# Attention probabilities of a hybrid trunk layer normalised by a scaled copy on ScalarE in place of VectorE's product

## The reference, cut to what matters

```python
s_lat = jnp.einsum('bcqhd,bckhd->bchqk', qb, k_blk) + bias      # 256 latent keys of the block
s_lat = jnp.where(mask, s_lat, NEG_INF)
s_ctx = jnp.einsum('bcqhd,bphd->bchqp', qb, k_ctx)              # 128 context keys
p = jax.nn.softmax(jnp.concatenate([s_lat, s_ctx], axis=-1), axis=-1)
o = einsum(p[..., :n_keys], v_blk) + einsum(p[..., n_keys:], v_ctx)
```

## Time and profile before

| what | value |
|---|---|
| median of 3 runs | 1238.8 us (1236.86 to 1239.94) |
| the profiled execution, its own time | 1235.06 us |
| its span, first to last instruction | 1233.2 us |
| busy over the span: PE, DVE, ACT, POOL | 91%, 73%, 55%, 21% |
| mean granted TensorE clock | 0.955 of 2.4 GHz |
| PtHi L1040 / PtLo L1437 / products L1448 | 80 each, mean 446 / 498 / 749 ns |

### The profile page before, as it was taken

The page is one execution under the profiler, slowest core; times in us unless marked ns, Lnnn a source line. Parts: engine busy times, 40 slices in busy tenths (PEclk is TensorE's granted clock), DMA queues, the critical chain, the costliest instruction groups (busy, mean ns, idle before and its releaser), DMA issues.

```text
span 1233.2 us, 19783 instructions
## 1 busy us (share of the span) xinstructions
PE 1120.8 (91%) x7082; PEld 1029.5 (83%) x7082; DVE 901.2 (73%) x1253; ACT 680.3 (55%) x1039; POOL 260.3 (21%) x139
## 2 busy tenths in 40 slices
PE   5899999989998999969999999995999999999950
PEld 1598988989898989969999999994788888888840
DVE  5738696968777696756556655737799999999928
ACT  3645747566666657552222222435578777877814
POOL 0232221222122221223333333211011101110011
PEclk9999999999999999979999999996899999999985
DMA  9235412211121112114433325618799999999945
GB/s 370 80 112 169 135 39 78 69 54 62 64 81 56 61 54 77 57 42 154 146 136 136 136 102 210 236 35 329 265 361 423 410 423 402 416 413 422 372 136 204
DMA packets 54569, 232.17 MB, mean 188 GB/s; under 512 B 5328, under 2 KB 22000, under 8 KB 46064
## 3 DMA queue, kind: packets, MB, share of 16 engines
q1 hardware_dynamic: 50480, 216.79, 46.6%
q0 software_dynamic: 4032, 14.68, 3.1%
HBM read 210.45 MB, written 21.00 MB: 188 GB/s over the span
## 4 chain that ended last, share of the span: by engine, by line
PE 48%; DVE 4%; DMA 1%; ACT 1%; issue 1%; POOL 0%; DVEq 0%; POOLq 0%; SPq 0%; ACTq 0%
PE PS L927 24%; PE PS L704 20%; PE PS L919 1%; PE PS L802 1%; PE PS L844 1%; DMA hS<-h_rows,idxI 1%; PE PS L940 1%; DVE xo L1924 1%; DVE xo L1926 1%; DVE hrow L1757 0%; DMA G<-slot_rows,slotI 0%; DVE yo L1936 0%; POOL wLo L598 0%; DVE WgLo L1860 0%; PE PS L832 0%
## 5 line engine op out<-in xcount | busy, mean ns | idle before, releaser
L598 POOL TENSOR_TENSOR wLo<-wRaw,wHi 128x1024 fp32r<-128x1024 f32 x80 | 205.7, 2571 | 573.7 <-ACT wHi L1004 573.7
L704 PE MATMUL PS<-hHi,wHi 128*128 128x320 f32 x896 | 286.6, 320 | 6.2 <-issue 2.5
L704 PE MATMUL PS<-hLo,wHi 128*128 128x320 f32 x896 | 279.1, 311 | 0.0
L704 PE MATMUL PS<-hHi,wLo 128*128 128x320 f32 x896 | 278.8, 311 | 0.0
L704 PEld LDWEIGHTS PS<-hHi,wHi 128*128 128x128 f32 x896 | 171.4, 191 | 6.9 <-issue 6.7
L704 PEld LDWEIGHTS PS<-hLo,wHi 128*128 128x128 f32 x896 | 170.8, 191 | 0.0
L704 PEld LDWEIGHTS PS<-hHi,wLo 128*128 128x128 f32 x896 | 170.3, 190 | 0.0
L1581 DVE SCALAR_TENSOR_TENSOR acc<-adaL,csil,acc 128x512 f32<-128x512 f32 x112 | 104.5, 990 | 9.6 <-DMA adaL<-in_w_ada_late 9.1
L1004 ACT ACTIVATE wHi<-wRaw 128x1024 fp32r<-128x1024 f32 x80 | 84.0, 1050 | 46.7 <-PE PS L704 46.7
L1860 DVE TENSOR_TENSOR WgLo<-Wg,WgHi 128x2048 fp32r<-128x2048 f32 x34 | 76.4, 2287 | 14.3 <-ACT WgHi L1219 14.3
L1437 DVE TENSOR_TENSOR PtLo<-PS,PtHi 128x384 fp32r<-128x384 f32 (+1 forms) x80 | 39.9, 498 | 60.6 <-ACT PtHi L1040 60.3
(11 more groups left out here) (324 smaller groups left out, 2791.8 us busy)
## 6 DMA issues: line engine op xcount, KB each, us to landing
wRaw<-in_wtiles SPq DMA_DIRECT2D x80, 512.0 KB, 3.4
Wu<-in_experts SPq DMA_DIRECT2D x18, 2048.0 KB, 9.7
Wg<-in_experts SPq DMA_DIRECT2D x18, 2048.0 KB, 9.8
Wd<-in_experts SPq DMA_DIRECT2D x17, 2048.0 KB
adaL<-in_w_ada_late SPq DMA_DIRECT2D x32, 512.0 KB, 4.2
slot_rows<-Ys SPq DMA_DIRECT2D x18, 512.0 KB, 10.6
ada<-in_w_ada SPq DMA_DIRECT2D x8, 1024.0 KB, 17.9
slot_rows<-tab SPq DMA_DIRECT2D x10, 512.0 KB, 6.6
```

The source lines that it names most:

```text
L598: nc.gpsimd.tensor_tensor(wLo[b][:], wRaw[b][:], wHi[b][:].bitcast(F32), ALU.subtract).then_inc(w_lo, 1)
L704: r = mm(PS[:, bank, 0:HALF], w[:, k, :], x[:, k, cols], start=(k == 0 and w is wHi[b] and x is xh), stop=(k == KT - 1 and w is wLo[b]))
```

## The change

The two products of a block leave VectorE. VectorE keeps the reciprocal, which now counts up a semaphore `prec_ok`; it waits until the copies of the block before are done, since they read the same `prec`. ScalarE waits for `prec_ok` and makes two copies in place with the reciprocal as scale. They stand in even stages between PtHi (L1040) and the weight copy (`high`). TensorE waits for `prob_ok` as before. VectorE has one ordered step less per block, and the semaphore `tab_zero` is folded into `ones_ok`.

```diff
--- before.py
+++ after.py
@@ -289,7 +289,7 @@
     half_mm, half_ev = sem("half_mm"), sem("half_ev")
     ones_ok, x2_in, sx_ok, xs_ok = sem("ones_ok"), sem("x2_in"), sem("sx_ok"), sem("xs_ok")
     bias_in, lw_hi, lw_lo, ada_ev = sem("bias_in"), sem("lw_hi"), sem("lw_lo"), sem("ada_ev")
-    tab_zero, spill_zero = sem("tab_zero"), sem("spill_zero")
+    spill_zero = sem("spill_zero")
     ada0_mm, xn_ok, ada_tp = sem("ada0_mm"), sem("xn_ok"), sem("ada_tp")
     row0_mm, row0_ok, adaV_ok = sem("row0_mm"), sem("row0_ok"), sem("adaV_ok")
     csil_ok, amul_ok = sem("csil_ok"), sem("amul_ok")
@@ -304,6 +304,7 @@
     u_hi, u_lo, qk_lo, v_hi = sem("u_hi"), sem("u_lo"), sem("qk_lo"), sem("v_hi")
     gate_sq, gate_z, gate_th = sem("gate_sq"), sem("gate_z"), sem("gate_th")
     vt_mm, v_ok, kt_mm, k_ok, kv_out = sem("vt_mm"), sem("v_ok"), sem("kt_mm"), sem("k_ok"), sem("kv_out")
+    prec_ok = sem("prec_ok")
     tab_ok, qk_mm, score_ok, exp_ok = sem("tab_ok"), sem("qk_mm"), sem("score_ok"), sem("exp_ok")
     prob_ok, pt_mm, pt_hi, pt_lo = sem("prob_ok"), sem("pt_mm"), sem("pt_hi"), sem("pt_lo")
     pv_mm, ya_ok = sem("pv_mm"), sem("ya_ok")
@@ -435,7 +436,7 @@
                     .then_inc(raw_in[(q + c) % 2], 16)
                 if project:
                     if c == 2 and isinstance(i, int) and i == 1:
-                        sp.wait_ge(tab_zero, 1)
+                        sp.wait_ge(ones_ok, 2)
                         for t in range(E, NT):
                             sp.dma_start(yd[t * P:(t + 1) * P, :].rearrange("p (x c) -> p x c", c=P),
                                          tab[:, 0, 0, 256:384].unsqueeze(1).broadcast_to([P, KT, P])) \
@@ -589,7 +590,7 @@
         for hh in range(2):
             for ty in range(3):
                 x = nc.gpsimd.memset(tab[:, hh, ty, 256:384], 0.0)
-        x.then_inc(tab_zero, 1)
+        x.then_inc(ones_ok, 1)
 
         def low(n, b):
 
@@ -893,7 +894,7 @@
 
         to_rows(0, xa, range(2 * TT))
 
-        pe.wait_ge(ones_ok, 3)
+        pe.wait_ge(ones_ok, 4)
         pe.wait_ge(g2T_ok, 1)
         pe.wait_ge(ohs_ok, 1)
         mm(PS[:, 5, 0:TT * E], triH[:], ohsH[:], start=True, stop=False)
@@ -1039,6 +1040,13 @@
                         nt = 1 if blk == 0 else 3
                         A(PtHi[:, 0:nt, hh * P:(hh + 1) * P], PS[:, 6, 0:nt * P].rearrange("p (t q) -> p t q", q=P),
                           ACT.Copy).then_inc(pt_hi, 1)
+                f = attention(i, s, 2, q)
+                if f:
+                    a, blk, b, pair = f
+                    act.wait_ge(prec_ok, a + 1)
+                    for hh in range(2):
+                        x = Sb[(blk + b) % 2][hh][:, 0:P if blk == 0 else 384]
+                        A(x, x, ACT.Copy, scale=prec[:, hh:hh + 1]).then_inc(prob_ok, 1)
                 if s % 2 == 0 and (project or s < 8):
                     c = s // 2
                     cur[0] = 5 * m + (5 * q + c + 1) // 2 + 1
@@ -1441,11 +1449,8 @@
                     a, blk, b, pair = f
                     w = P if blk == 0 else 384
                     dve.wait_ge(exp_ok, 2 * a + 2)
-                    st(v.reciprocal(prec[:], psumr[:]))
-                    seq.last()
-                    for hh in range(2):
-                        x = Sb[(blk + b) % 2][hh][:, 0:w]
-                        v.tensor_scalar(x, x, prec[:, hh:hh + 1], None, ALU.mult).then_inc(prob_ok, 1)
+                    wait(dve, prob_ok, 2 * a)
+                    v.reciprocal(prec[:], psumr[:]).then_inc(prec_ok, 1)
                 f = attention(i, s, 1, q)
                 if f:
                     a, blk, b, pair = f
@@ -1552,8 +1557,8 @@
                     if k == KT - 1:
                         x.then_inc(ylo_ok, 1)
 
-        dve.wait_ge(tab_zero, 1)
-        iterations(nc.vector, iteration, seq, 2 * 24)
+        dve.wait_ge(ones_ok, 2)
+        iterations(nc.vector, iteration, seq, 2 * 19)
 
 
         dve.wait_ge(ya_ok, 2 * BLOCKS * KT)
```

## The result

| | before | after |
|---|---|---|
| median | 1239.14 us (1236.86 to 1239.94, 4 runs) | 1268.72 us (1264.39 to 1272.75, 4 runs) |
| ratio | | 1.0245, 95% interval 1.022 to 1.0269 |
| profiled execution, span | 1235.06, 1233.2 us | 1267.83, 1266.0 us |
| busy PE, DVE, ACT over the span | 1120.8, 901.2, 680.3 us | 1128.1, 827.1, 721.8 us |
| mean granted clock | 0.955 | 0.945 |

The kernel is 29.6 us slower. Slower was forecast, by 18.5 us; the median lies 0.7 us above the range. Nearly all of it arises before the merge: TensorE starts its first merge matmul (L704 of before, L705 here, with yrHi) at 541.56 us before and at 573.32 after, 31.8 us later; the rest of the span is 1.0 us longer (these two profiled executions differ by 32.8 us, the medians by 29.6).

What follows compares the result with a forecast made beforehand. TensorE was taken as the bound, waiting on PtLo at stage 1. Terms 10.9 (stage 0) + 1.8 (iteration 8) + 3.0 (tail) + 2.8 (clock) = 18.5 us gave 1257.3 us on the 1238.8 median, range 1246 to 1268.

Steps and rivals of the forecast that it cites:

- What bounds the kernel, and the chain of stage 0: TensorE bounds; in stage 0 the chain through ScalarE's lwHi to PtLo grows 1.82 us, 10.9 us over iterations 2 to 7.
- Iteration 8 and the tail: Iteration 8's stage 0 chain costs 1.8 us; two more blocks normalised in tail stages 8 and 10 cost 3.0 us.
- The other even stages: Even stages besides stage 0: ScalarE is 1.8 us late but catches up in idle time, cost 0.
- Rival 1: Copies delay VHi in stage 4, so TensorE waits on kLo in seven iterations: 8.8 us more, 1266 us, chance 0.17.
- The clock, 2.8 us: After stage 1 waits, 2.5 more clock falls at 1.1 us each cost 2.8 us, bounds 0 and 5.
- Rival 2: VectorE's freed time between PtHi of stage 0 and PtLo of stage 1 counts: faster, about 1228 us, chance 0.03.
- rivals 3 and 4: Part of the delay covered, 11.1 us, 1250 (chance 0.14); no bite in stage 0, tail's 3.0 us only, 1241.8 (0.04).
- GpSimd's share in VectorE's busy time: About 23 of the products' 56.6 us is VectorE blocked by GpSimd; gain off the chain, next instruction may be blocked instead.

Runs made afterwards that it cites:

- e2_stage0: Kernel before, with only block 4 of each head pair, normalised in stage 0, scaled on ScalarE: 1257.19 us, ratio 1.0178.
- e12_ti: Kernel before, with the evacuating tanh of the fourth LRU product (ti) moved from ScalarE's stage 0 to stage 1: 1221.87 us, ratio 0.9884.
- e3_stage8: Kernel before, with only block 3, normalised in stage 8, scaled on ScalarE: 1248.68 us, ratio 1.0107.
- e4_rest: Kernel before, with only blocks 0, 1 and 2, normalised in stages 2, 4 and 6, scaled on ScalarE: 1238.33 us, ratio 1.0022.
- e6_fill: Changed kernel, with 32 idle matmuls in front of TensorE's wait at stage 1 of iterations 2 to 7: 1255.94 us, ratio 1.0166 against before.
- e9_hybrid: Changed kernel, with copies at the end of ScalarE's even stages in iterations 1 to 7, products on VectorE in iteration 8 and tail: ratio 1.0015 against before.
- e14: Kernel before, with ti in stage 1, copies ending ScalarE's even stages in iterations 1 to 7, products on VectorE in iteration 8: 1230.18 us, ratio 0.9958.
- e1: Changed kernel, with plain copies that neither wait for the reciprocal nor scale by it: 1248.13 us, ratio 1.0102 against before.
- e5: Changed kernel, with the wait and scaled copies moved to the end of ScalarE's even stage: 1245.28 us, ratio 1.0083 against before.
- e10: Kernel before, with copies ending ScalarE's even stages in iterations 1 to 7 and VectorE's two long LRU instructions moved to stage 1: ratio 1.0051.
- e13: Changed kernel, with ti moved from ScalarE's stage 0 to stage 1: 1258.43 us, ratio 1.0191 against before.
- e7: Kernel before, with 20 idle matmuls in front of TensorE's wait at stage 1 of iterations 2 to 7: 1234.26 us, ratio 1.0001.

## Why the prediction was right or wrong

- **What bounds the kernel, and the chain of stage 0**: right. The 1.82 us forecast for ScalarE's chain came out at 1.83 in four iterations and 1.82 in the eighth, made of 0.80 for the reciprocal and 1.03 for two copies of 609 ns (611 forecast). The place of the first failure apart, the forecast's terms for waits, 10.9 + 1.8 + 3.0 = 15.7 us, came out at 12.8 + 2.9 = 15.7. e2_stage0 and e12_ti confirm it from both sides.
- **Iteration 8 and the tail**: 1.8 and 2.9 us, for 1.8 and 3.0.
- **"The other even stages ... there it idles before the next PtHi or evacuation and catches up ... Cost 0"**: wrong, this is the first step that failed. In stage 8 the copies also stand in front of ti, with 0.6 us of room before TensorE needed it. It cost 7 x 1.11 = 7.8 us. e3_stage8 has it without the waits of stage 0. For stages 2, 4 and 6 the zero was right (e4_rest). I had looked where ScalarE waits; what had to be looked at was, for each instruction behind the new ones, how long before its reader it ended.
- **Rival 1**, a second wait in each of seven iterations for 8.8 us: the size was near, the place and the cause were not. kLo never held TensorE; the wait was ScalarE's ti. Its chance, 0.17, was too small: of all that stood behind the copies I had priced the slack of kLo alone.
- **The clock, 2.8 us**: the mechanism was right and the term mis-sized, the second failure. It measured 7.7 us in the six iterations and 7.5 by the two runs with filled pauses; 7.0 is what the waits leave of the whole first part. I took the number of falls as what would change and their cost as fixed at 1.1 us. The falls at stage 1 went from four to seven, for 6.5 expected, but those behind 4.5 us and more cost 1.3 to 2.5 us each, 2.0 in the mean (1.9 by e6_fill).
- **The loop's edge**, 1.3 us in iterations 4 and 6, was in no term. Before, too, these two waited longer (3.30 and 3.14 against 2.69); the excess grew.
- Sum: 12.8 + 1.3 + 7.8 + 2.9 + 7.0 = 31.8, for 18.5 forecast. The 7.0 is a remainder and makes the sum come out by construction; its parts are 7.7, 1.5 and -2.1, the last a pause in iteration 1 that the change does not touch. The 13.3 us that the forecast lacks are 7.8 of ti, 1.3 at the loop's edge and 4.2 of clock.
- **Rival 2** (VectorE's freed time counts) is refuted by e9_hybrid; **rivals 3 and 4** by the stage 1 waits.
- **GpSimd's share in VectorE's busy time**: VectorE's busy time in the first part fell by 71.0 us (343.12 to 272.12), 56.6 of products and 14.4 more. The prediction feared that the next VectorE instruction would meet the same GpSimd instruction, and this is what the rows show, with a gain besides. One of the three taps of the convolution u now takes 2.9 us in seven iterations, each time beside a wLo (its line went from 18.7 to 32.8 us busy), while others that had met one before no longer do: cLo 18.4 to 2.8 us (mean 2630 to 404 ns), the copy prm 10.0 to 1.2, g 12.0 to 6.6. None of it was on TensorE's path, as the sum had assumed.

## What to carry to other kernels

Before work is moved to an engine, list every instruction that will stand behind it in that engine's queue, and for each the time from its end to the start of its reader on the bound engine; the smallest of these, not the engine's idle share, is what the move may take. An operand that another engine makes late in the same stage adds a wait of its own (0.80 us here, against 1.03 for the work itself), so the new work belongs behind everything that is urgent, where both costs vanished in iterations 1 to 7 (in the tail they did not, and with another order of VectorE's the late copies held up PtHi of the next stage). A pause of TensorE costs more than its length when the clock falls behind it, which cuts both ways: 0.8 us taken from a chain that seven iterations wait for gave 1.2%, some 0.1 of it perhaps the luck of the build.

## What was not expected of the hardware

- The time that a fall of the clock costs grew with the pause, but only in the mean. Over the 8 us behind a wait at stage 1 the time lost, 8 x (1 - mean clock), was 0 in two cases and 1.4 to 1.7 us in four behind 2.69 to 3.30 us of waiting (before), 1.5 to 3.0 behind 4.5 to 5.8 (after), and 0 behind the six of 1.87 to 2.60 (e12_ti). The other runs show how loose this is: 1.71 behind 1.87 us in one of e14's four, 0 behind one of the four of 3.52 in e1, 1.71 behind 4.98 in e2.
- At the turn of the hardware loop an engine can stand up to 3.2 us with no releaser in the rows. TensorE stood 2.56 to 3.22 us at one or both of the turns to iterations 4 and 6 in e2, e3, e4, e5, e9, e10, e13 and e14, 1.26 to 1.58 in e6 and e7, and next to nothing in the other six, before and after among them. ScalarE stood 1.39 to 1.40 in after and e1, 1.56 and 1.70 in e14. In iteration 1, where nothing turns, TensorE pauses at 111 to 113 us in every build, for 1.18 to 2.57 us. The instructions there were the same in kind; it differs from one build to the next, and its cause stays open. Part of a pause comes off the wait that follows: 2.56 + 1.68 and 2.80 + 1.19 us in e4_rest, where before waited 3.30 and 3.14. Even so it makes differences of 3 us between builds of this kernel hard to put down to their edits.
